# A two-block transformer kernel: score and output matmuls of two 64-wide heads issued alternately

## The reference

```python
for l in range(2):
    h = rmsnorm_2(x, norm_mix[l]);  proj = h @ w_in[l]
    # A, B, C, each head of width 64 over 256 tokens:
    s = q @ k.T * 64**-0.5 (+ bias, mask);  p = softmax(s, axis=-1);  o = p @ v
    x = x + concatenate([rmsnorm_2(oa), rmsnorm_2(ob), rmsnorm_2(oc)]) @ w_o[l]
    u = relu(rmsnorm_2(x, norm_mlp[l]) @ w_up[l]);  x = x + (u * u) @ w_down[l]
```

## Time and profile before

| | us |
|---|---|
| runs | 3490.22, 3492.25, 3498.49 |
| median | 3492.25 |
| profiled execution | 3494.03 |
| its span, first to last instruction | 3492.4 |
| mean granted clock of TensorE | 0.970 |

### The profile page before, as it was taken

How to read it: one execution, slowest core, us unless ns; L and a number is a source line. 1 busy time by engine, 2 the same in 40 slices (tenths; PEclk the granted TensorE clock), 3 DMA queues, 4 the chain that set the end, 5 groups by cost and what they waited for, 6 DMA issues and landing times.

```text
span 3492.4 us, 63817 instructions
## 1 busy us (share of the span) xinstructions
PE 3306.4 (95%) x27350; PEld 3203.3 (92%) x27350; DVE 2265.7 (65%) x2517; ACT 1429.8 (41%) x1418; POOL 158.2 (5%) x292
## 2 busy tenths in 40 slices
PE   5999978999999998989999999999998999999998
PEld 5998878999999997878999999998877999999998
DVE  5888868565665675567655555557566855555555
ACT  3343333344444443444533333334344543333333
POOL 2111101000000000011000000000001000000000
PEclk6899988999999999999999999999999999999999
DMA  9888868655555543334555555555433455555553
GB/s 377 293 294 319 295 229 295 201 193 192 192 193 192 193 161 118 118 121 143 188 194 194 193 194 194 193 182 158 132 104 127 154 188 193 193 193 194 193 194 134
DMA packets 320750, 681.70 MB, mean 195 GB/s; under 512 B 14768, under 2 KB 21620, under 8 KB 320164
## 3 DMA queue, kind: packets, MB, share of 16 engines
q1 hardware_dynamic: 286272, 562.74, 48.4%
q0 software_dynamic: 31232, 109.07, 8.5%
q10 hardware_dynamic: 3108, 7.89, 0.6%
HBM read 677.47 MB, written 7.94 MB: 196 GB/s over the span
## 4 chain that ended last, share of the span: by engine, by line
PE 83%; DVE 9%; DMA 4%; issue 2%; ACT 2%; POOL 0%; ACTq 0%; DVEq 0%; POOLq 0%; SPq 0%
PE G L655 49%; PE Dn L655 33%; DVE w_lo L1162 2%; PE Dn L658 1%; DVE ada_acc L1282 1%; DMA ada_raw<-in_w_ada 1%; DMA raw<-in_w_in 1%; ACT w_hi L2022 1%; DMA zT<-in_w_ada 1%; DMA raw<-in_w_out 1%; DVE sq L1206 0%; DVE negmax L1558 0%; DVE xT L1820 0%; DVE s_sb L1555 0%; DVE s_sb L1551 0%
## 5 line engine op out<-in xcount | busy, mean ns | idle before, releaser
L655 PE MATMUL G<-h_hi,w_hi 128*128 128x256 f32 x5760 | 1626.4, 282 | 26.1 <-DVE w_lo L1162 13.6
L2022 ACT CAST w_hi<-raw 128x2048 fp32r<-128x2048 f32 (+2 forms) x536 | 1016.9, 1899 | 1470.5 <-DMA raw<-in_w_down 430.0
L655 PE MATMUL G<-h_lo,w_hi 128*128 128x256 f32 x5760 | 1612.2, 280 | 0.0
L655 PE MATMUL G<-h_hi,w_lo 128*128 128x256 f32 x5760 | 1611.5, 280 | 0.0
L1162 DVE TENSOR_TENSOR w_lo<-raw,w_hi 128x2048 fp32r<-128x2048 f32 (+2 forms) x536 | 1219.1, 2274 | 571.2 <-ACT w_hi L2022 569.8
L655 PEld LDWEIGHTS G<-h_hi,w_hi 128*128 128x128 f32 x5760 | 1100.5, 191 | 39.9 <-issue 21.6
L655 PEld LDWEIGHTS G<-h_lo,w_hi 128*128 128x128 f32 x5760 | 1099.8, 191 | 0.4
L655 PEld LDWEIGHTS G<-h_hi,w_lo 128*128 128x128 f32 x5760 | 1099.0, 191 | 0.0
L655 PE MATMUL Dn<-act_hi,w_hi 128*128 128x256 f32 x2752 | 762.2, 277 | 7.4 <-DVE act_lo L1674 7.4
L655 PE MATMUL Dn<-act_lo,w_hi 128*128 128x256 f32 x2752 | 761.7, 277 | 0.0
L655 PE MATMUL Dn<-act_hi,w_lo 128*128 128x256 f32 x2752 | 761.6, 277 | 0.0
(11 more groups left out here) (239 smaller groups left out, 1650.3 us busy)
## 6 DMA issues: line engine op xcount, KB each, us to landing
raw<-in_w_up SPq DMA_DIRECT2D x128, 1024.0 KB, 5.3
raw<-in_w_down SPq DMA_DIRECT2D x128, 1024.0 KB, 5.0
raw<-in_w_in SPq DMA_DIRECT2D x88, 1024.0 KB, 5.2
ada_raw<-in_w_ada POOLq DMA_DIRECT2D x152, 512.0 KB, 6.4
raw<-in_w_ffn_gate SPq DMA_DIRECT2D x44, 1024.0 KB, 5.0
raw<-in_w_ffn_up SPq DMA_DIRECT2D x44, 1024.0 KB, 5.0
raw<-in_w_ffn_down SPq DMA_DIRECT2D x44, 1024.0 KB, 5.0
raw<-in_w_o SPq DMA_DIRECT2D x32, 1024.0 KB, 5.1
```

The source lines that it names most:

```text
L655: return nc.tensor.matmul(o, lhsT, rhs, start=start, stop=stop, skip_group_check=True)
L2022: s.copy(w_hi[j][:, 0:PIECE_K * n], raw[j][:, 0:PIECE_K * n]).then_inc(hi_done, 1)
```

## The change

For a slot that starts two heads, the transposes of both finished heads now come first; then both heads' waits, and then the score matmuls in the order head 0 t 0, head 1 t 0, head 0 t 1, head 1 t 1. For a slot that finishes two heads, the waits of both outputs come first, and the output matmuls alternate in the same way. Slots with single heads and the first block's heads (kind F) are issued as before. No instruction is added or removed.

```diff
+            def score_pair(new, base):
+                for H, kind, h in new:
+                    score_waits(kind, h, base + H)
                 for t in range(QT):
-                    i = mm(SC[H % 2][:, t, :], zT[r0:r0 + 64, qt_, t * P:(t + 1) * P], zT[r0:r0 + 64, kt_, :],
-                           t == 0, t == 1)
-                i.then_inc(qk_done, 1)
+                    for H, kind, h in new:
+                        i = score(H, kind, h, t)
+                        if t == QT - 1:
+                            i.then_inc(qk_done, 1)
 
             def slot(done, new, base):
 
+                pair = len(new) == 2
                 for n in range(max(len(done), len(new))):
                     if n < len(done):
                         H, kind, h = done[n]
                         finish(H, kind, h, base + H, 0)
-                    if n < len(new):
+                    if n < len(new) and not pair:
                         H, kind, h = new[n]
                         scores(H, kind, h, base + H)
-                if done:
+                if pair:
+                    score_pair(new, base)
+                if len(done) == 2:
                     misc_open(out_name(done), mbase[0])
                     for H, kind, h in done:
-                        i = finish(H, kind, h, base + H, 1)
+                        out_waits(kind, h, base + H)
+                    for k in range(QT):
+                        for H, kind, h in done:
+                            i = out_mm(H, kind, h, k)
                     i.then_inc(misc_w, 1)
+                elif done:
+                    misc_open(out_name(done), mbase[0])
+                    H, kind, h = done[0]
+                    finish(H, kind, h, base + H, 1).then_inc(misc_w, 1)
```

More of the change, by code:

```diff
@@ L812, in finish, with out_waits @@
                     return
+                out_waits(kind, h, no)
+                for k in range(QT):
+                    i = out_mm(H, kind, h, k)
+                return i
+            def out_waits(kind, h, no):
                 pe.wait_ge(pt_copied, no + 1)
@@ L815, in finish, with out_mm @@
                     pe.wait_ge(v_turned, h + 1)
+                else:
+                    pe.wait_ge(v_turned, lay[0] * len(V2_TILES) + (HEADS1 + v_need(kind, h)[1]))
+            def out_mm(H, kind, h, k):
+                if kind == "F":
                     o, v = MISC, v_tok[:, :, h * P:(h + 1) * P]
                 else:
-                    c, need = v_need(kind, h)
-                    pe.wait_ge(v_turned, lay[0] * len(V2_TILES) + (HEADS1 + need))
+                    c = v_need(kind, h)[0]
                     o = MISC[64 * (h % 2):64 * (h % 2) + 64, :]
                     v = v_tok[:, :, c:c + 64]
-                for k in range(QT):
-                    i = mm(o, v[:, k, :], pT[H % 2][:, k, :], k == 0, k == QT - 1)
-                return i
+                return mm(o, v[:, k, :], pT[H % 2][:, k, :], k == 0, k == QT - 1)
             def scores(H, kind, h, no):
@@ L836, in scores, with score_waits @@
                     return
+                score_waits(kind, h, no)
+                for t in range(QT):
+                    i = score(H, kind, h, t)
+                i.then_inc(qk_done, 1)
+            def score_waits(kind, h, no):
                 pe.wait_ge(exp_done, no - 1)
@@ L844, in scores, with score @@
                         pe.wait_ge(swap_done, lay[0] * 3 + 3)
+            def score(H, kind, h, t):
                 r0 = 64 * (h % 2)
                 qt_, kt_ = qk_tiles(kind, h)
+                return mm(SC[H % 2][:, t, :], zT[r0:r0 + 64, qt_, t * P:(t + 1) * P], zT[r0:r0 + 64, kt_, :],
+                          t == 0, t == 1)
+            def score_pair(new, base):
+                for H, kind, h in new:
+                    score_waits(kind, h, base + H)
                 for t in range(QT):
-                    i = mm(SC[H % 2][:, t, :], zT[r0:r0 + 64, qt_, t * P:(t + 1) * P], zT[r0:r0 + 64, kt_, :],
-                           t == 0, t == 1)
-                i.then_inc(qk_done, 1)
+                    for H, kind, h in new:
+                        i = score(H, kind, h, t)
+                        if t == QT - 1:
+                            i.then_inc(qk_done, 1)
             def slot(done, new, base):
+                pair = len(new) == 2
                 for n in range(max(len(done), len(new))):
```

## The result

| | before | changed |
|---|---|---|
| median of 20 runs, us | 3494.76 | 3504.28 |
| lowest to highest, us | 3490.22 to 3506.92 | 3495.79 to 3513.16 |
| ratio of the times | | 1.0024, 95% interval 1.0014 to 1.0033 |
| profiled execution: time, span, mean clock | 3494.03, 3492.4, 0.970 | 3503.14, 3501.5, 0.967 |

The changed kernel is slower by 0.24%, 5 to 12 us (8.4 us by the ratio, 9.5 by the medians). Of these 2 us, and of the 9 us between forecast and median, 2.5 us are the kernel before itself, whose median of 20 runs is 3494.76 where the three runs shown had 3492.25. The rest is not: the forecast was 2.6 us slower, and the change made it about 8 to 9 us slower.

The account below looks back on a forecast made before the run. TensorE, 95% busy, was taken to bound the kernel. Per layer -1.05 + 1.42 + 0.8 + 0.15 = +1.3 us, two layers +2.6 us on the median 3492.25, gave 3494.9 us; 8-in-10 range 3488 to 3502 us.

Parts of the forecast that it names:

- rivals A and B: All 20 pairs: A, no overlap today, alternation gains 36 us, 3%; B, alternation breaks the overlap, costs 36 us, 6%.
- Step 1: Score and output pairs already neighbours: alternating them changes 0 us, since eight records already take the time of four.
- Step 2: Slots finishing two and starting two heads, seven a layer: 4.25 us becomes 4.04, a gain of 0.21 us per slot.
- Step 3: First head's scores start 1.42 us later, delaying VectorE: costs 1.42 us a layer at p = 33, 0.8 at p = 39.
- rival C: VectorE's delay is hidden at p = 33 and 39 too; all 14 slots keep 0.21 us: 3489.6 us, 12%.
- Step 4: Outputs at p = 27, 34, 40: first head waits for second's copy; end moves 0.05 us, three times a layer.
- rival D: TensorE's clock falls in the longer wait at p = 34: 2 us a layer taken, 3499 us, 25%.

Follow-up runs that it names:

- not alternated: Changed kernel with the two inner loops swapped, so all matmuls of head 0 precede head 1's, scores and outputs: 3505.18 us, ratio 1.0027 to before.
- C slots alone: Kernel before with the change only in slots finishing or starting C heads (p = 21 to 27): 3491.62 us, ratio 0.9989 to before.
- B and A slots only: Kernel before with the change only in slots p = 28 to 40: 3502.81 us, ratio 1.0019 to before.
- scores ahead: Kernel before with a pair's scores together between the two transposes, or ahead of them in six waiting slots: 3486.02 us, ratio 0.9971 to before.
- the filled pair: Changed kernel and kernel before, each with 14 extra score matmuls a layer ahead of transposes in five slots: 3494.16 and 3493.37 us.

## Why the prediction was wrong, step by step

- What bounds the kernel, and that the pairs overlap already: right. Eight records took 1.07 us before, alternated, and not alternated again, so rivals A and B are out.
- Step 1, alternation at 0 us: right, by the kernel not alternated.
- Step 2, a C slot 0.21 us shorter: measured 0.25. C slots alone made the kernel faster.
- Step 3, the second block later by 1.42 us at p = 33 and about 0.8 at p = 39: at full clock 1.39 and 0.63. The mechanism and the size hold, and rival C (this delay is hidden) is out.
- Step 4, 0.05 us for outputs behind a common wait, 0.1 at most: mis-sized, 0.20 us (first record 0.26 us behind the copy's end). Six of them, 0.9 us more than counted. The row that I took the 0.05 from was an output behind outputs, where the new order has an output behind transposes.
- The step that failed is the clock. The sum has no term for it, that is 0; rival D kept it apart with a chance of 25%, looked for it at one place only, p = 34, and priced it at 2 us a layer. That the clock might fall in longer waits was the right mechanism. Measured: in the profile of the changed kernel it fell at p = 33 and 36 of both layers and at p = 40 of one, none of them the place I had named, and cost 3.8 to 4.0 us a layer between p = 33 and 37 alone. At p = 34 it fell in one layer of two in the kernel not alternated and in that with B and A slots only.
- The rule by which I placed it was too simple. I compared single waits (2.16 us that cost the clock, 1.44 that did not). In these runs 1.88 us cost it and 2.09 did not, and at p = 36, behind a wait that hardly changed (1.44 to 1.64 us in all profiles without fill or scores ahead), it fell in five of the six layers with the new B and A order and in none of the eight with the old. What the change adds is waits close to each other: 0.77 us for PT inside each slot with two pairs, and the longer one in front of p = 34. At p = 33 two waits of 0.77 us stand 1.4 us apart in all six layers, but the clock fell inside that slot only in the two of the changed kernel. That the order brings the falls and that work in the waits removes them is shown; which combination of waits it takes is not.
- Over all 20 runs the mean clock is 0.9670 against 0.9697 and 0.9703 in the two groups of before, some 0.003 lower: 0.003 x 3500 = 10 us is the most that can cost. Within the runs of before the time rises by 1.1 to 1.8 us for each 0.001, which would make 3 to 6 us (an estimate: the clock of a run is given to 0.001 only).
- So the sum: 2.6 us of waits as forecast, 0.9 us more for the outputs, and for the clock 3 to 6 us by the runs, some 6 by the filled pair, 7.7 by the one profile. With 3 to 6 it makes 6.5 to 9.5 us; measured 8.4 (5 to 12). Had the three runs of before been as slow as the later 20, the range would have reached just past the measured time; that would have been luck, since the term that is missing is larger than the whole forecast.

## What to carry to other kernels

Before counting on matmuls in two halves of the array to overlap, look in the timeline whether two neighbours already do; here the whole intended gain was there. When blocks are moved together to make neighbours, ask what the moved block covered (a copy) and who was waiting for it (VectorE), and move instead the block that another wait can hide. A wait added to TensorE next to others can cost more than its length, by the clock that falls with it: here 1.4 to 1.6 us of waits a layer cost 5.4. Useful work put into the wait gives back both. And a control that adds work has to be looked through slot by slot: the same fill that costs nothing in a long wait costs its full time behind a short one.

## What the hardware showed that was not expected

- Matmuls of two heads in different halves of the array start beside each other even when all four records of one stand ahead of the other's in the list: eight records in 1.07 us alternated, in 1.07 us in line (p = 32 before), and one head alone in 1.06.
- A first output record behind a wait started 0.26 us after the copy's end where transposes ran before it (p = 27 changed), and 0.05 us after it where other outputs did (p = 27 before). That the change from the 128-column to the 64-column form makes the difference is a guess from these two places; no run tested it.
- Fourteen more matmuls a layer in waits made the changed kernel 10 us faster, and the clock between p = 33 and 37 went from 0.89 to 1.00.
